# Rotated queries of the last attention, turned by VectorE and moved through DRAM instead of transposed by TensorE

## The chip, the cores and the metric

The kernel runs on one core of one Trainium2 chip. The metric is the device time of one execution in microseconds (us); the number given for a kernel is the median of its runs. The core's engines work side by side and meet at semaphores: TensorE (PE) multiplies and transposes, VectorE (DVE) and ScalarE (ACT) do elementwise work, SyncE (SP) issues almost all DMAs. Each engine takes its own instructions in the order in which they were written, and an instruction that waits holds up everything behind it on that engine.

## The reference

A float32 network over 256 tokens of width 2048, batch 1. Block one: gated linear attention and dilated attention side by side, an output projection and a gated feed-forward. Block two has two layers: retention with a convolution, then sliding-window attention with sinks. The change touches the attention of that last layer:

```python
q, k, v, gate = jnp.split(proj, ...)                 # proj = h @ w_in, 32 query heads of 64, 4 key/value heads
q = rope(rms_norm_2(q.reshape(b, s, 32, 64), q_norm_w), pos)
k = rope(rms_norm_2(k.reshape(b, s, 4, 64), k_norm_w), pos)
scores = q @ k^T * 64**-0.5                          # keys of the own 128-token block (causal) and the one before (window 128)
m = max(max(scores), sink); p = exp(scores - m); p = p / (sum(p) + exp(sink - m))
x = x + (p @ v * silu(gate)) @ w_out
```

## The kernel before

**The stream of products.** Nearly all the work is products of 256 tokens with about 340 MB of float32 weights. Each operand is cut into a high and a low part, and three products replace one. A *unit* is two k-tiles of 128 rows by 512 columns. For each unit SP loads 512 KB into one of four raw buffers, ACT writes the high part (`wh`, line 1408), DVE the low part (`wl`, line 1688), and PE runs 12 matmuls (lines 1218 to 1220), in two halves of six. There are three buffers for `wh`/`wl`: ACT can cut unit u+2 only once PE has finished unit u-1, that is when it starts unit u, and PE needs both parts two units later.

**One order for all engines.** The class `Plan` writes a single list of steps. It inserts the side work (norms, rotations, attention, splitting of activations) as *lanes*, generators that advance by half a unit (`SLOT`); `room`, `made` and `free` hold a lane back, for at most six half-units, until the planner's own table `WORK` says that an engine is free or a result is there. Each engine then walks the same list and issues its own part of each step. The list is fixed before the kernel runs; the semaphores only make an engine wait. `cut u` stands two units ahead of `mul u`.

**The last attention.** 32 query heads are worked in eight *quads* g = 0 to 7 of four heads; block j = g // 2 of the query projection (`oq`) feeds two quads. For block j:

- `oq_evac`, `on_sq` (ACT): out of PSUM into `TW`, and its squares.
- `on_rope j k` (DVE): rotation of token block k = 0, 1, three operations of 128x512 each.
- `oq_turn j k` (PE lines 1237 to 1242, ACT line 1663 on): four PE transposes of 128x128 into a bank `m`, and a copy by ACT into `qo` (in `A1`).
- `on_sum j`, `on_root j` (DVE): the sums of squares and the inverse roots by Newton steps, which scale the scores.

For quad g: `oqk g` (PE, line 1265: scores of four heads into the three `m` banks and `ob`; DVE adds the mask), `omax g` (DVE), `oexp g i` (ACT, i = 0 to 3), `oapt g i` (PE transposes the probabilities of two heads, ACT copies them, DVE makes two masked parts; i = 0, 1), `oapv g` (PE, into `ob`; ACT copies it out), `ogate g` (DVE: silu(gate) times 1/sum). The silu itself is `og j` (ACT), once per block j of the gate projection. Silu and exponential use different tables of ACT, and a change between them is an ACT_TABLE_LOAD.

The gate of a quad is turned without PE: `turn` (DVE, line 1784) transposes 32x32 pieces, `send` (SP, line 2295, four DMAs of 64 KB) writes them to a DRAM tensor `blocks`, `fetch` (SP, line 2302, one DMA of 256 KB) reads them back in the right places, and the step `msent M5 2g` multiplies with the attention's output (DVE), writes the high part `mh` (ACT) and then the low part `ml` (DVE). SP holds at a `send` until the turn is done and at a `fetch` until its four sends have landed. The output projection's units read `mh`/`ml`: unit 645 needs quad 4's, 646 quad 5's, 647 quad 6's, and 651 quad 7's. Units 629 to 644 read quads 0 to 3.

In short: the three uses of the `m` banks (`oq_turn`, `oqk`, `oapt`) take the banks in turn, and `ob` serves one head of `oqk` and all of `oapv`.

Of the kernel before, what the change touches and what calls it, by code (L numbers as in the profile page):

```python
# [103 lines left out]
def all_units(blocks):  # L104
# [15 lines left out]
    for u, un in enumerate(units):  # L120
# [28 lines left out]
        "ok_dup": (0, .8, 0), "ok_turn": (.6, 0, .45), "oq_turn": (.6, 0, .45), "og": (1.27, 0, 0)}  # L149
# [3 lines left out]
class Plan:  # L153
# [8 lines left out]
    def __init__(self, blocks, units):  # L162
        self.order, self.said, self.there, self.norms, self.emptied = [], set(), {}, 0, set()
        self.lanes = {"first": [], "att": [], "fin": [], "gate": [], "post": []}
        self.pause = dict.fromkeys(self.lanes, 0)
        self.now, self.through, self.end = 0.0, {"act": 0.0, "dve": 0.0}, {}
        self.turns, self.own, self.place, self.before = [], 0, {}, {}
        self.ring = []
        self.blocks, self.units = blocks, units
        self.lay()  # L170

    def say(self, *p):
# [23 lines left out]
        if p[0] in ("oq_turn", "oapt", "oqk"):  # L196
            self.ring += [p] * (3 if p[0] == "oqk" else 1)
# [110 lines left out]
    def after(self, b):  # L308
# [93 lines left out]
        elif kind == "oq":  # L402
# [29 lines left out]
    def turned_and_sent(self, *p):  # L432
# [11 lines left out]
        self.spawn(self.fetched(p))  # L444

# [206 lines left out]
def program(nc, t, out):  # L652
# [22 lines left out]
    by_act = ("apt", "g_kturn", "ok_turn", "oq_turn", "oapt")  # L675
# [43 lines left out]
    assert plan.turns == [q[1:] for q in plan.order if q[0] == "turn"] == list(sents)  # L719
# [10 lines left out]
    with ctx:  # L730
# [202 lines left out]
        qo = A1[:, 0:2048].rearrange("p (r h t) -> p r h t", r=2, h=4)  # L933
# [92 lines left out]
        def turn_places(p):  # L1026

            n, (group, i) = (sents[p] - 1) % 2, plan.place[p]
            if group == "r":
                return PB[:, :, 256:384], A2[:, 5128:5640].rearrange("p (i n) -> p i n", i=4)  # L1030
            first, then = {"d": (A2[:, 4096:5120], A2[:, 5120:6144]), "o": (A2[:, 2560:3584], A2[:, 3584:5632]),
# [13 lines left out]
        def sent(p):  # L1045

            n = sents[p] - 1
            return s_send[n % 2], 64 * (n // 2 + 1)

        def back(p):  # L1050

            n = sents[p] - 1
# [5 lines left out]
        def turn_place_free(p):  # L1058

            kind = p[3] if p[0] == "msent" else p[1]  # L1060
# [45 lines left out]
        def turn_source(p):  # L1106

            if p[0] == "xsent":
# [7 lines left out]
        def turn_ready(p):  # L1116

            if p[0] == "xsent":
                return x_ready(int(p[1][1]), p[2] // 4)
# [8 lines left out]
        def aw_free(*p):  # L1128
# [3 lines left out]
            return (s_turn, sents[before[-1][1:]]) if before else (s_bank, 0)  # L1132
# [13 lines left out]
        def tensor(e):  # L1146
# [8 lines left out]
            for p in plan.order:  # L1155
# [81 lines left out]
                elif kind == "oq_turn":  # L1237
                    on.wait_ge(s_orope, nth("on_rope", *a))
                    on.wait_ge(*bank_free(*p))
                    o, k = bank(*p), a[-1]  # L1240
                    four(lambda c: o[:, 128 * c:128 * c + 128],
                         lambda c: T3[:, k, 128 * c:128 * c + 128]).then_inc(s_bank, 1)
# [22 lines left out]
                elif kind == "oqk":  # L1265
                    g, j = a[0], a[0] // 2
                    on.wait_ge(*moved("oq_turn", j, 1))
                    on.wait_ge(*moved("ok_turn", 1))
                    for i in range(3):
                        on.wait_ge(*bank_free("oqk", g, i))  # L1270
                    on.wait_ge(ob_by[ob_free[p][0]], ob_free[p][1])
                    for i in (0, 2):
                        heads = [(od_bank(g, n), qo[rows_of(n), j % 2, 2 * (g % 2) + n // 2, :],
                                  ko[rows_of(n), j, :]) for n in (i, i + 1)]
                        for o, q, k in heads:
                            e.matmul(o[:, 0:128], q[:, 0:128], k[:, 0:128], start=True, stop=True)  # L1276
                        for n, (o, q, k) in enumerate(heads):
                            e.matmul(o[:, 128:384], q[:, 128:256], k[:, 0:256], start=True,  # L1278
# [118 lines left out]
        def scalar(e):  # L1397
# [18 lines left out]
            for p in plan.order:  # L1416
# [219 lines left out]
                elif kind in ("ok_evac", "oq_evac"):  # L1636
# [5 lines left out]
                    else:  # L1642
                        on.wait_ge(s_dup, 2)
                        if a[0]:
                            on.wait_ge(*full("oq_turn", a[0] - 1, 1))
# [13 lines left out]
                elif kind == "ok_turn":  # L1659
# [3 lines left out]
                         bank(*p)[:, :].rearrange("p (h t) -> p h t", h=4)).then_inc(s_bank_act, 1)  # L1663
                elif kind == "oq_turn":
                    j, k = a
                    on.wait_ge(*full(*p))
                    on.wait_ge(s_sent, sents[last_sent("xsent", "X3")])
                    if j >= 2:
                        on.wait_ge(s_pv, opened[("oqk", 2 * (j - 2) + 1)])
                    copy(qo[:, j % 2, :, 128 * k:128 * k + 128],  # L1670
# [11 lines left out]
        def vector(e):  # L1682
# [33 lines left out]
            for p in plan.order:  # L1716
# [57 lines left out]
                elif kind == "turn":  # L1774
                    n, (to, _) = sents[a], turn_places(a)
# [6 lines left out]
                    for i, part in enumerate(parts):  # L1782
                        m = slice(2 * i, 2 * i + 2) if len(parts) == 2 else slice(0, 4)
                        last = e.transpose(to.rearrange("p i (m n) -> p m i n", n=32)[:, m],
# [458 lines left out]
        def sync(e):  # L2243
# [24 lines left out]
            for p in plan.order:  # L2268
# [19 lines left out]
                elif kind == "send":  # L2288
                    n = sents[a] - 1
# [7 lines left out]
                elif kind == "fetch":  # L2297
                    n, (_, to) = sents[a] - 1, turn_places(a)
                    on.wait_ge(*sent(a))
                    if plan.before[a]:  # L2300
# [101 lines left out]
```

## Time and profile before

| | us |
|---|---|
| median of 3 runs | 1885.65 (1883.7 to 1885.96) |
| the profiled execution, whole time | 1886.98 |
| its span in the trace | 1885.1 |
| PE busy | 1876.4 (100% of the span) |
| DVE busy | 1256.0 (67%) |
| ACT busy | 996.8 (53%) |
| DMA, share of 16 engines in queue q1 | 65.0% |
| granted PE clock, mean | 0.999 |

PE's records overlap: one matmul of 128x512 is shown with 390 ns, but the next starts 0.227 us later. The starts, not the durations, give PE's pace. A gap between starts that is wider than this is time that the engine lost.

### The profile page before, as it was taken

How to read it: one execution, taken by the hardware profiler on the slowest of the kernel's cores; microseconds unless marked ns; L12 is line 12 of the kernel's file. 1: busy time of each engine (PE TensorE's matmuls, PEld its weight loads, DVE VectorE, ACT ScalarE, POOL GpSimd, SP SyncE). 2: the span in 40 equal slices, each digit the busy share in tenths (PEclk: the TensorE clock that was granted, in tenths of full speed). 3: DMA queues.
4: the chain of work that ended last, by engine and by line, in shares of the span. 5: the costliest groups of instructions: out<-in, count | busy, mean ns of one | idle time of the engine just before them, and what ended most of it. 6: DMA issues, size and time to landing. Idle time of an engine off the chain costs nothing.

```text
span 1885.1 us, 22394 instructions
## 1 busy us (share of the span) xinstructions
PE 1876.4 (100%) x8531; PEld 1545.0 (82%) x8531; DVE 1256.0 (67%) x1837; ACT 996.8 (53%) x1370; POOL 14.4 (1%) x32
## 2 busy tenths in 40 slices
PE   9999999999999999999999999999999999999999
PEld 7888888888888888888888888888888888877777
DVE  5676566776666466665466776765776676777875
ACT  6677554554444444443444465654555555566663
POOL 0001000000000000000000000000000000000000
PEclk9999999999999999999999999999999999999999
DMA  9767764686666666665666686666666577655555
GB/s 314 209 194 179 208 182 151 217 251 195 192 194 194 192 190 191 199 195 194 192 193 195 209 276 197 191 192 187 190 204 195 193 245 226 188 167 149 182 186 177
DMA packets 212362, 375.96 MB, mean 199 GB/s; under 512 B 14672, under 2 KB 35968, under 8 KB 212256
## 3 DMA queue, kind: packets, MB, share of 16 engines
q1 hardware_dynamic: 211008, 371.78, 65.0%
q0 software_dynamic: 816, 2.11, 0.8%
q8 instruction: 67, 1.10, 0.2%
q10 hardware_dynamic: 432, 0.66, 0.1%
q14 instruction: 39, 0.32, 0.0%
HBM read 361.89 MB, written 12.60 MB: 199 GB/s over the span
## 4 chain that ended last, share of the span: by engine, by line
PE 98%; DVE 1%; DMA 1%; ACT 0%; issue 0%; SPq 0%; DVEq 0%
PE g L1218 31%; PE g L1220 31%; PE g L1219 31%; PE m L1152 1%; PE ob L1296 0%; PE m L1278 0%; DMA A<-blocks 0%; DMA raw<-in_w_in 0%; PE m L1378 0%; PE m L1276 0%; PE m L1264 0%; PE ob L1364 0%; DVE wl L1688 0%; PE ob L1299 0%; PE m L1308 0%
## 5 line engine op out<-in xcount | busy, mean ns | idle before, releaser
L1688 DVE TENSOR_TENSOR wl<-raw,wh 128x1024 fp32r<-128x1024 f32 (+1 forms) x660 | 802.3, 1217 | 546.5 <-ACT wh L1408 543.2
L1408 ACT ACTIVATE wh<-raw 128x1024 fp32r<-128x1024 f32 (+1 forms) x661 | 695.0, 1052 | 721.2 <-PE g L1220 712.7
L1218 PE MATMUL g<-wh,xh 128*128 128x512 f32 x1886 | 741.7, 393 | 3.1 <-DVE wl L1688 2.7
L1220 PE MATMUL g<-wh,xl 128*128 128x512 f32 x1886 | 735.2, 390 | 0.0
L1219 PE MATMUL g<-wl,xh 128*128 128x512 f32 x1886 | 734.7, 390 | 0.0
L1218 PEld LDWEIGHTS g<-wh,xh 128*128 128x128 f32 x1886 | 354.5, 188 | 82.2 <-DVE wl L1688 5.0
L1220 PEld LDWEIGHTS g<-wh,xl 128*128 128x128 f32 x1886 | 354.3, 188 | 74.2
L1219 PEld LDWEIGHTS g<-wl,xh 128*128 128x128 f32 x1886 | 354.6, 188 | 72.1
L1218 PE MATMUL g<-wh,mh 128*128 128x512 f32 x732 | 287.6, 393 | 0.0
L1220 PE MATMUL g<-wh,ml 128*128 128x512 f32 x732 | 285.1, 389 | 0.0
L1219 PE MATMUL g<-wl,mh 128*128 128x512 f32 x732 | 284.9, 389 | 0.0
L1218 PEld LDWEIGHTS g<-wh,mh 128*128 128x128 f32 x732 | 137.4, 188 | 29.5 <-issue 1.6
L1220 PEld LDWEIGHTS g<-wh,ml 128*128 128x128 f32 x732 | 137.4, 188 | 28.8
L1219 PEld LDWEIGHTS g<-wl,mh 128*128 128x128 f32 x732 | 137.5, 188 | 28.1
L1826 DVE STREAM_TRANSPOSE A<-A 32x256 f32<-32x256 f32 x176 | 76.7, 436 | 2.9
L1688 DVE TENSOR_TENSOR x<-g,x 128x512 f32<-128x512 f32 (+1 forms) x73 | 46.4, 677 | 13.2 <-PE g L1220 7.9
L1405 ACT ACTIVATE A<-g,st 128x512 f32<-128x512 f32 x50 | 31.6, 683 | 31.3 <-PE g L1220 31.3
L1408 ACT ACTIVATE A<-TW 32x256 f32<-32x256 f32 x96 | 39.9, 416 | 1.5
L1691 DVE SCALAR_TENSOR_TENSOR xl<-A,small,xh 128x128 fp32r<-128x128 f32 (+1 forms) x112 | 34.1, 363 | 7.0 <-ACT xh L1408 7.0
L1408 ACT ACTIVATE mh<-A 128x512 fp32r<-128x512 f32 (+1 forms) x42 | 21.9, 540 | 21.1 <-DVE A L1826 16.4
L1408 ACT ACTIVATE xh<-A,small 128x256 fp32r<-128x256 f32 x64 | 28.7, 494 | 2.0 <-DMA A<-blocks 2.0
L1688 DVE TENSOR_TENSOR ml<-A,mh 128x512 fp32r<-128x512 f32 (+1 forms) x42 | 23.8, 582 | 6.8 <-ACT mh L1408 6.8
(186 smaller groups left out, 758.1 us busy)
## 6 DMA issues: line engine op xcount, KB each, us to landing
raw<-in_ev_w_in SPq DMA_DIRECT2D x128, 512.0 KB, 3.9
raw<-in_w_in SPq DMA_DIRECT2D x92, 512.0 KB, 4.3
raw<-in_w_gate SPq DMA_DIRECT2D x88, 512.0 KB, 4.4
raw<-in_w_up SPq DMA_DIRECT2D x88, 512.0 KB, 4.4
raw<-in_w_down SPq DMA_DIRECT2D x88, 512.0 KB, 4.6
raw<-in_od_w_in SPq DMA_DIRECT2D x72, 512.0 KB, 4.0
raw<-in_w_out SPq DMA_DIRECT2D x32, 512.0 KB, 4.1
raw<-in_ev_w_out SPq DMA_DIRECT2D x32, 512.0 KB, 4.7
```

The lines of the kernel that those rows point to most:

```text
L1152: last = e.transpose(dst(c), src(c), ident)
L1218: e.matmul(o, hi[:, kt, c], h, start=first, stop=False)
L1219: e.matmul(o, hi[:, kt, c], l, start=False, stop=False)
L1220: last = e.matmul(o, lo[:, kt, c], h, start=False, stop=end)
L1405: return e.activation(o, i, func, scale=scale, bias=bias)
L1408: return e.activation(o, i, AF.Copy, scale=scale)
L1688: return e.tensor_tensor(o, a, b, op)
L1691: return e.scalar_tensor_tensor(out=o, in0=a, scalar=s, in1=b, op0=op0, op1=op1)
L1826: last = e.transpose(dst, src)
```

## The change

The step `oq_turn` is gone. The rotated queries now take the way of the gates: a new pair `turn` / `send` of kind `qsent j k` behind each `on_rope j k`, and a `fetch` of at least four half-units later, straight into `qo`. This `fetch` has no splitting step behind it. DVE writes the 32x32 pieces in such an order that `qo` holds, for each token block, the four groups of heads interleaved (`p (i n)` with `n = 4n' + m`): `oqk` reads its 128 query columns of one group with a step of four elements. Sends and fetches of both kinds share the numbering of `blocks` and its semaphores (`turned_n` in place of `sents`).

Around it: `on_sum` and `on_root` of a block stand behind the second `turn`. In `oqk`, PE waits for both fetches, for banks 0 and 1 ahead of the first two heads, and for bank 2 and `ob` only ahead of the last two. In the planner, `oqk` holds until the fetch is in the list, its estimated landing (2.4 us) is over, and the previous user of `ob` is done (at most eight half-units); `oapv` holds for the previous user of `ob` as well; `og` asks for room on ACT.

```diff
-        "ok_dup": (0, .8, 0), "ok_turn": (.6, 0, .45), "oq_turn": (.6, 0, .45), "og": (1.27, 0, 0)}
+        "ok_dup": (0, .8, 0), "ok_turn": (.6, 0, .45), "og": (1.27, 0, 0)}
...
+        if p[0] in ("oqk", "oapv"):
+            self.ob = p
...
                 say("on_rope", a[0], k)
-            for k, p in enumerate(("on_sum", "on_root")):
-                yield 2 if k else 1
-                yield from self.made("on_rope", a[0], k)
-                say("oq_turn", a[0], k)
+                if k:
+                    self.sent_in_place(a[0], 0)
+            yield 1
+            yield from self.room("dve", 1.0)
+            self.sent_in_place(a[0], 1)
+            for p in ("on_sum", "on_root"):
+                yield 1
                 yield from self.room("dve", 1.0)
                 say(p, a[0])
...
             assert kind == "og"
+            yield from self.room("act", .6)
             say("og", a[0], b.i)
...
+    def sent_in_place(self, j, k):
+
+        p = ("qsent", j, k)
+        self.say("turn", *p)
+        self.say("send", *p)
+        self.place[p], self.before[p] = ("q", 0), None
+        self.turns.append(p)
+        self.spawn(self.fetched_in_place(p))
+
+    def fetched_in_place(self, p):
+
+        yield 4
+        self.say("fetch", *p)
+        self.end[("fetch",) + p] = self.now + 2.4
+        yield 1
...
     def od_quad(self, g):
         say = self.say
+        while ("fetch", "qsent", g // 2, 1) not in self.said:
+            yield 1
         for _ in range(8):
-            if (all(self.end[p] <= self.now for p in [("oq_turn", g // 2, 1)] + self.ring[-3:]) and
+            if (all(self.end[p] <= self.now for p in [("fetch", "qsent", g // 2, 1)] + self.ring[-3:] +
+                    [self.ob] * (g > 0)) and
                     self.through["dve"] - self.now <= 1.0):
                 break
             yield 1
...
+        yield from self.made(*self.ob)
         say("oapv", g)
...
                 elif kind == "oqk":
                     g, j = a[0], a[0] // 2
-                    on.wait_ge(*moved("oq_turn", j, 1))
+                    for k in range(2):
+                        on.wait_ge(*back(("qsent", j, k)))
                     on.wait_ge(*moved("ok_turn", 1))
-                    for i in range(3):
-                        on.wait_ge(*bank_free("oqk", g, i))
-                    on.wait_ge(ob_by[ob_free[p][0]], ob_free[p][1])
                     for i in (0, 2):
-                        heads = [(od_bank(g, n), qo[rows_of(n), j % 2, 2 * (g % 2) + n // 2, :],
+                        if i == 2:
+                            on.wait_ge(ob_by[ob_free[p][0]], ob_free[p][1])
+                        for n in (0, 1) if i == 0 else (2,):
+                            on.wait_ge(*bank_free("oqk", g, n))
+                        heads = [(od_bank(g, n), [qo[rows_of(n), j % 2, k].rearrange("p i (n m) -> p m (i n)", m=4)
+                                                  [:, 2 * (g % 2) + n // 2] for k in range(2)],
                                   ko[rows_of(n), j, :]) for n in (i, i + 1)]
...
-                elif kind == "oq_turn":
-                    j, k = a
-                    on.wait_ge(*full(*p))
...
+                        order = "p i (n m) -> p m i n" if a[0] == "qsent" else "p i (m n) -> p m i n"
```

The whole order of the stage moves with it. Three places are shown; line numbers of the changed kernel are about 31 higher.

**SP, around the first gate's way through DRAM** (`blocks<-A2` are the sends, `A2<-blocks` the fetch of quad 0's gate, `raw` the weight loads). Before:

```order
L1144 DMA raw<-in_od_w_in 128x2x512 [waits s_lo] x40
L2295 DMA blocks<-A2 32x4x128 [waits s_fetch0,s_turn]
L2295 DMA blocks<-A2 32x4x128 x3
L1144 DMA raw<-in_od_w_in 128x2x512 [waits s_lo] x2
L2302 DMA A2<-blocks 128x512 [waits s_send0]
```

And of the change:

```order
L2319 DMA blocks<-A2 32x4x128 [waits s_fetch0,s_turn]
L2319 DMA blocks<-A2 32x4x128 x3
L1178 DMA raw<-in_od_w_in 128x2x512 [waits s_lo] x2
L2319 DMA blocks<-A2 32x4x128 [waits s_fetch1,s_turn]
L2319 DMA blocks<-A2 32x4x128 x3
L2330 DMA A2<-blocks 128x512 [waits s_send0]
```

The sends of `qsent 2 0`, which wait for their own turn on DVE, now stand between the gate's sends and its fetch.

**ACT, at the silu of gate block 2** (`A2<-g` is `og 2`, `bias<-m0` and `A1<-m` copies out of the `m` banks, `mh<-` the step `msent`, `PB` and `st` the exponentials). Before:

```order
L1408 ACTIVATE A1<-m2 128x4x128 [waits s_bank]
L1408 ACTIVATE wh<-raw 128x1024 [waits s_mul,s_raw2]
L1405 ACT_TABLE_LOAD [waits s_gated]
L1405 ACTIVATE A2<-g0,st 128x512 [waits s_mul]
L1405 ACTIVATE A2<-g1,st 128x512
L1408 ACTIVATE wh<-raw 128x1024 [waits s_raw3]
```

And of the change:

```order
L1439 ACTIVATE mh<-AW 128x512 [waits s_oprod]
L1439 ACTIVATE wh<-raw 128x1024 [waits s_mul,s_raw3]
L1436 ACT_TABLE_LOAD
L1436 ACTIVATE A2<-g0,st 128x512 [waits s_gated]
L1436 ACTIVATE A2<-g1,st 128x512
L1439 ACTIVATE bias<-m0 128x512 [waits s_bank]
L1439 ACTIVATE wh<-raw 128x1024 [waits s_mul,s_raw0]
```

The silu now stands behind `msent M5 4` (which needs quad 2's fetch) and ahead of the copy of `oapt 3 1`, for which PE's `oapv 3` waits.

**PE, at the end of the attention** (`ob<-` is `oapv 7`). Before; the first matmul of `g0` belongs to unit 645:

```order
L1296 MATMUL ob<-PT,A1 64x256 [waits s_ob_act,s_masked]
L1296 MATMUL ob<-PT,A1 64x256
L1299 MATMUL ob<-bias,A1 64x128 x2
L1296 MATMUL ob<-bias,A1 64x256 x2
L1299 MATMUL ob<-bias,A1 64x128 x2
L1218 MATMUL g0<-wh,mh 128x512 [waits s_read_dve,s_sent,s_lo]
```

And of the change; here it belongs to unit 647:

```order
L1327 MATMUL ob<-PT,A1 64x256 [waits s_ob_act,s_masked]
L1327 MATMUL ob<-PT,A1 64x256
L1330 MATMUL ob<-bias,A1 64x128 x2
L1327 MATMUL ob<-bias,A1 64x256 x2
L1330 MATMUL ob<-bias,A1 64x128 x2
L1252 MATMUL g0<-wh,mh 128x512 [waits s_sent,s_lo]
```

Quad 7 is two units later against the products. Quad 6's `fetch` moved from behind the first half of unit 642 to behind the first half of unit 645, and its `msent` from unit 644 to directly ahead of unit 647.

## Rows read from the trace of the kernel before

**Rows 1.** The page: engines' busy time, and the two costliest groups of DVE and ACT.
```profile
PE 1876.4 (100%) x8531; PEld 1545.0 (82%) x8531; DVE 1256.0 (67%) x1837; ACT 996.8 (53%) x1370; POOL 14.4 (1%) x32
...
L1688 DVE TENSOR_TENSOR wl<-raw,wh 128x1024 fp32r<-128x1024 f32 (+1 forms) x660 | 802.3, 1217 | 546.5 <-ACT wh L1408 543.2
L1408 ACT ACTIVATE wh<-raw 128x1024 fp32r<-128x1024 f32 (+1 forms) x661 | 695.0, 1052 | 721.2 <-PE g L1220 712.7
```

**Rows 2.** Waits of PE: engine, line, releaser: total us, times, longest.
```profile
PE g L1218 <- DVE wl L1688: 2.7, 2, 2.4
...
PE m L1276 <- ACT PT L1408: 0.9, 1, 0.9
```

**Rows 3.** Timeline of PE around one `oq_turn`: start, us, engine, line.
```profile
1624.85 0.39 PE L1220 MATMUL g<-wh,xl 128*128 128x512 f32 x1
1625.08 0.60 PE L1152 MATMUL m<-small,TW 128*128 128x128 f32 x4
...
1629.62 0.39 PE L1218 MATMUL g<-wh,xh 128*128 128x512 f32 x1
```

**Rows 4.** Timeline of PE: the long gap, and an `oqk` without one.
```profile
1703.67 0.39 PE L1220 MATMUL g<-wh,xl 128*128 128x512 f32 x1
1706.44 0.50 PE L1218 MATMUL g<-wh,xh 128*128 128x512 f32 x1 [2.38 <-DVE wl L1688]
...
1709.19 0.63 PE L1219 MATMUL g<-wl,xh 128*128 128x512 f32 x1
...
1712.38 0.49 PE L1276 MATMUL m<-A 64*128 64x128 f32 x4 [0.89 <-ACT PT L1408]
...
1713.89 0.50 PE L1218 MATMUL g<-wh,xh 128*128 128x512 f32 x1
...
1735.48 0.39 PE L1220 MATMUL g<-wh,xl 128*128 128x512 f32 x1
...
1737.31 0.50 PE L1218 MATMUL g<-wh,xh 128*128 128x512 f32 x1
```

**Rows 5.** Timeline of ACT at `og 1`: silu's table load and evacuation.
```profile
1701.63 1.28 ACT L1405 ACT_TABLE_LOAD   x1
1702.92 1.26 ACT L1405 ACTIVATE A<-g,st 128x512 f32<-128x512 f32 x2
```

**Rows 6.** Timeline of DVE: `omax`, quad 6's `msent`, quad 7's `turn`.
```profile
1696.06 1.21 DVE L1697 TENSOR_REDUCE st<-PB 128x8 f32<-128x1024 f32 x1
...
1836.42 0.75 DVE L1688 TENSOR_TENSOR AW<-AW,A 128x256 f32<-128x256 f32 x2
1837.87 0.69 DVE L1688 TENSOR_TENSOR ml<-AW,mh 128x512 fp32r<-128x512 f32 x1 [0.70 <-ACT mh L1408]
...
1841.85 0.71 DVE L1784 STREAM_TRANSPOSE A<-AW 128x512 f32<-128x512 f32 x1
```

**Rows 7.** Timeline of SP: quad 6's fetch, quad 7's four sends.
```profile
1830.70 0.41 SPq L2302 DMA_DIRECT2D A<-blocks  x1
...
1842.59 1.78 SPq L2295 DMA_DIRECT2D blocks<-A  x4
```

**Rows 8.** DMA issues at 1691 us, quad 0's fetch: KB each, us to landing.
```profile
A<-blocks SPq DMA_DIRECT2D x1, 256.0 KB, 3.9
```

**Rows 9.** DMA issues from 1842 us: quad 7's sends, then its fetch.
```profile
blocks<-A SPq DMA_DIRECT2D x4, 64.0 KB, 2.9
...
A<-blocks SPq DMA_DIRECT2D x1, 256.0 KB, 5.3
```

**Rows 10.** Timeline of PE: units 642, 649, 650 and 651 begin.
```profile
1827.60 0.40 PE L1218 MATMUL g<-wh,mh 128*128 128x512 f32 x1
...
1848.81 0.39 PE L1218 MATMUL g<-wh,mh 128*128 128x512 f32 x1
...
1851.53 0.39 PE L1218 MATMUL g<-wh,mh 128*128 128x512 f32 x1
...
1854.40 0.47 PE L1218 MATMUL g<-wh,mh 128*128 128x512 f32 x1
```

More of the change, by code:

```diff
@@ L195, in say @@
             self.norms += 1
-        if p[0] in ("oq_turn", "oapt", "oqk"):
+        if p[0] in ("oqk", "oapv"):
+            self.ob = p
+        if p[0] in ("oapt", "oqk"):
             self.ring += [p] * (3 if p[0] == "oqk" else 1)
@@ L673, in find @@
         return next(p for p in plan.order if p[:len(start)] == start)
-    by_act = ("apt", "g_kturn", "ok_turn", "oq_turn", "oapt")
+    by_act = ("apt", "g_kturn", "ok_turn", "oapt")
     by_dve = ("xturn", "mix", "gates", "bias", "aqk", "g_gate", "g_at", "g_state", "r_s")
@@ L718, in program @@
     sents = {p: n + 1 for n, p in enumerate(q for q in plan.order if q[0] in ("xsent", "msent"))}
-    assert plan.turns == [q[1:] for q in plan.order if q[0] == "turn"] == list(sents)
+    assert plan.turns == [q[1:] for q in plan.order if q[0] == "turn"]
+    assert [p for p in plan.turns if p[0] != "qsent"] == list(sents)
+    turned_n = {p: n + 1 for n, p in enumerate(plan.turns)}
     ropes = {p: n + 1 for n, p in enumerate(q for q in plan.order if q[0] == "eq_rope")}
@@ L1058, in turn_place_free @@
         def turn_place_free(p):
-            kind = p[3] if p[0] == "msent" else p[1]
+            kind = {"msent": p[3:4], "xsent": p[1:2], "qsent": ("o",)}[p[0]][0]
             if kind == "d":
@@ L1106, in turn_source @@
         def turn_source(p):
+            if p[0] == "qsent":
+                return [T3[:, p[2], 0:512]]
             if p[0] == "xsent":
@@ L1116, in turn_ready @@
         def turn_ready(p):
+            if p[0] == "qsent":
+                return s_orope, nth("on_rope", p[1], p[2])
             if p[0] == "xsent":
@@ L1131, in aw_free @@
                       if q[:2] == ("turn", "msent")]
-            return (s_turn, sents[before[-1][1:]]) if before else (s_bank, 0)
+            return (s_turn, turned_n[before[-1][1:]]) if before else (s_bank, 0)
         def weights(e, u):
@@ L1236, in tensor @@
                          lambda c: src(c % 2, c // 2)).then_inc(s_bank, 1)
-                elif kind == "oq_turn":
[L1238 to L1242, printed above, removed]
                 elif kind == "bias":
@@ L1644, in scalar @@
                         if a[0]:
-                            on.wait_ge(*full("oq_turn", a[0] - 1, 1))
+                            on.wait_ge(s_turn, turned_n[("qsent", a[0] - 1, 1)])
                     evacuate(T3, b)
@@ L1783, in vector @@
                         m = slice(2 * i, 2 * i + 2) if len(parts) == 2 else slice(0, 4)
-                        last = e.transpose(to.rearrange("p i (m n) -> p m i n", n=32)[:, m],
+                        order = "p i (n m) -> p m i n" if a[0] == "qsent" else "p i (m n) -> p m i n"
+                        last = e.transpose(to.rearrange(order, n=32)[:, m],
                                            part.rearrange("p (m i n) -> p m i n", i=4, n=32))
@@ L2297, in sync @@
                 elif kind == "fetch":
-                    n, (_, to) = sents[a] - 1, turn_places(a)
+                    n, (_, to) = turned_n[a] - 1, turn_places(a)
                     on.wait_ge(*sent(a))
+                    if a[0] == "qsent":
+                        on.wait_ge(s_sent, sents[last_sent("xsent", "X3")])
+                        if a[1] >= 2:
+                            on.wait_ge(s_pv, opened[("oqk", 2 * (a[1] - 2) + 1)])
                     if plan.before[a]:
```

26 lines of the change are left out of this document (11 added, 15 removed).

## The prediction, written before the changed kernel ran

> **What bounds the kernel now.** I read the page first: PE is busy for 1876.4 of 1885.1 us, DVE 67%, ACT 53% [rows 1]. DVE's longest wait by far is for ACT's `wh`, and ACT's is for PE's matmuls [rows 1], so both run at PE's pace and PE's own work is the bound. Then PE's waits, which is where a changed order would show: in the whole run PE waited once for long on `wl` and once on ACT's copy `PT` [rows 2]. Then PE's timeline, for what one step costs. The starts are read there, since busy times overlap: units 649 and 650 begin 2.72 us apart [rows 10], 12 products with 0.227 us from start to start; I use 2.73 for a unit. Four transposes between 1624.85 and 1629.62 stretch 19 gaps (4.31 us) to 4.77 [rows 3]: a set of four costs 0.46 us.
>
> **Terms that make it faster.** (a) Eight sets of PE transposes go (four blocks, two halves each): 8 x 0.46 = 3.7 us, all on PE's path. Eight ACT copies of such a bank go too; ACT waits for PE most of the time, so I count nothing for them. (b) The stall of before. From 1703.67 to 1713.89 PE spent 10.22 us [rows 4]. In it lie 13 product gaps (2.95), four transposes (0.46) and one `oqk`. The `oqk` at 1735.48 shows what that costs without a wait: 1.83 us to the next product, less one gap, 1.60 [rows 4]. That makes 5.01, so 5.2 us are lost: 2.5 in the gap, the rest in products at the lower clock (0.43 us apart at 1709.19, the 1.2 GHz level, after an idle time of 2.38) and in `oqk` waiting for `PT`. Its cause is the order: `omax 2`, `on_root 2` and `msent 0` stand in one row on DVE, and behind it on ACT `mh`, silu's table and evacuation (1.28 + 1.26, [rows 5]) and only then `wh`. The new order takes `on_root 2` out of this row, and `oqk` no longer waits for bank 2 ahead of its first heads. I count the whole 5.2 as gone and the new order's own stalls below. Together -8.9 us.
>
> **What is added at no cost.** Eight `turn`s of 0.71 [rows 6] on DVE, 5.7 us in about 190, where DVE waits for ACT between most cuts; a turn is dear only where it delays something, and those places are priced below. Forty DMA issues on SP, 1.78 for four sends and 0.41 for a fetch [rows 7]: 8 x 2.2 = 17.5 us of SP, which otherwise waits for a free raw buffer. `oqk`'s new wait for its queries: the fetch stands at least three units (8.2 us) ahead of every `oqk` that needs it, and fetches land in 3.9 to 5.3 us [rows 8, 9]. Without this cover each of the four blocks' first quads would hold PE by up to 5 us.
>
> **Terms that make it slower.** Here I walk the new order at the three places where a chain through DRAM, DVE and ACT ends at PE. Rules: ACT can begin cut u+2 when PE begins unit u, PE needs it two units (5.5 us) later; a cut takes 1.05 on ACT and 1.22 on DVE [rows 1]; a rotation is three operations of 128x512, 0.69 each as the one that writes `ml`, `omax` a reduction of 1.21 and three small operations, about 1.7 [rows 6]; `ogate` about 1.3, exponentials of two parts about 1.05 (estimates from the same timelines). The same walk over the old order gives its stall as 2.8 us against the 2.5 seen, and no other.
>
> (c) *Quad 0's gate and `oapt 1 1`.* Zero is PE's start of unit 600; with `oapv 0` and `oapt 1 0` between, units 602, 605 and 607 start at 6.9, 15.6 and 21.0. DVE finishes cut 602 at 3.2, `omax 1` 4.9, `ogate 0` 6.2, the gate's turn 6.9, cuts 603 and 604 at 8.0 and 9.5, the rotation 11.6, the turn of `qsent 2 0` 12.2. SP must send that (1.8) before the gate's fetch, which goes out at 14.1 and lands at 17.9 to 19.4. DVE is ready for it at 16.9 and is held. Behind it in a row: the product 0.75, `mh` 0.65, `wh` of cut 607, silu 2.54, cut 608, exponential's table (another 1.28) and `oexp 1 3`: done at 26.6 or later. PE wants `oapt 1 1` at 23.8, so it idles 2.9 us, in two pieces. Then ACT's copy and DVE's masks (behind `on_sum 2`) come 1 us after PE wants `oapv 1`. With the mean landing I take 4.2. Bounds: 0, if the waits that I sum are met by slack that I don't see, and 7.3, with the slow landing and one period at the lower clock (1.9).
>
> (d) *Quad 2's gate and `oapv 3`.* Zero is the start of unit 614. The turn of `qsent 3 0` ends at 14.9, the gate's at 15.6; eight sends end at 18.5 and land 2.9 later [rows 9]; the fetch goes at 21.4 and lands at 25.2 to 26.7, while DVE could start at 23.9. Then product, `mh`, cut 623, silu with table, copy of `oapt 3 1`, masks: 0.75 + 0.65 + 1.05 + 2.54 + 0.6 + 0.76, with a little for the semaphores 6.6. So `oapv 3` can start at 32 to 33 and PE wants it at 28.7: 3.3 at the quick landing. One gap of this length is longer than the one that lowered the clock [rows 4], so I add its 1.9: 5.2. Bounds 0 and 6.5.
>
> (e) *The end.* Before, quad 6's fetch went out 3.1 us after unit 642 began (1827.60 to 1830.70), its `ml` was written at 1838.56: 11.0 us [rows 6, 7, 10]. In the new order the same chain starts from unit 645, and unit 647 needs its end. PE's way there is two units, `oapt 7 1` and `oapv 7`: 5.46 + 0.46 + 1.45 = 7.4. PE waits 3.6, or 1.8 with a landing of 3.9 instead of 5.3 [rows 8, 9]; I take 3.1. Quad 7's turn follows this step on DVE, 0.7 later. From the end of a turn to unit 651's start it was 1842.56 to 1854.40, 11.8 us [rows 6, 10]; PE's four units from 647 to 651 take 10.9. That leaves another 0.7 + 11.8 - 10.9 = 1.6. The clock may fall in the first wait, but the second then shrinks by as much. Sum 4.7, bounds 2.0 and 6.6 (DVE up to 1.4 behind at cut 647).
>
> **Sum.** -3.7 - 5.2 + 4.2 + 5.2 + 4.7 = +5.2 us. On the profiled execution's own time, 1886.98 (span 1885.1 and 1.9 around it), that is 1892.2; it ran 1.3 above the median, and on the median of 1885.65 the sum gives 1890.9. What this measurement can tell from no change is 0.2%, 3.8 us.
>
> **Rivals.**
> 1. *Faster, 1880.* DVE and ACT stay ahead of PE: (c) and (d) cost nothing because the exponentials and masks of a quad are done when PE arrives, and only the low end of (e) is paid: 1885.65 - 8.9 + 3.3. For it: PE met such a wait once in the old stage though DVE was just as full. Against it: in (c), even with the fetch landing at once, the silu and two table loads leave `oexp 1 3` 1.8 us late. It decides from (c) + (d) below 1.5 us; with (e) hidden as well 1876.8.
> 2. *No change, 1885.* The same stalls at half price: (c) 2.5, (d) 2, (e) 4 against 8.9. For it: my walk lets every duration be the full one, while packed operations on DVE start 0.1 before the last one's end is shown.
> 3. *Reading the queries with a step of four elements slows PE's weight loads.* No row shows a strided weight. An `oqk` is 16 matmuls whose loads lie side by side with them; if each load took twice as long, `oqk` would grow from 1.6 to at most 3.1, eight times: +12, to 1903. If strides cost nothing, 0, which the nearest row, the unstrided `oqk` of 1.60 [rows 4], leaves open. The Trainium skill (SBUF — State Buffer, the note on cachelines under its port mapping) says that SBUF has 16-byte lines and that each access to a new line pays; a step of four float32 is just such an access each time, although the same note calls four float32 still free. No row here decides that.
>
> **Chances.** My forecast (+3.8 to +10) 0.46; rival 1, 0.28; rival 2, 0.20; rival 3, 0.06. So faster 0.28, within 0.2% 0.20, slower 0.52. The likeliest case alone spans 1889.5 to 1896. The range has to reach into the faster case: 1879 leaves out the part of rival 1 in which (e) is hidden too, 1897 the strided reads, under 2 in 10 together.
>
> **What would show it.** Right: PE's `oqk` still about 1.6 us per quad; no stretch like 1703 to 1714 at `msent 0` with 5.2 us lost; PE idle before `oapt 1 1` and before `ob<-` of quads 1 and 3, released by ACT or by DVE's masks; PE idle at unit 647 on DVE's `ml`, 2 to 4 us, and again at 651; SP's fetch of quad 0's gate directly behind four sends. Wrong: PE's waits add up to under 5 us (rival 1); PE waits at `oqk` for DMA (the cover of three units failed); the PE weight loads of `oqk` longer than 0.19 us (rival 3); DVE's turn of a query well over 0.71 us.

## The result, and the profile after

| | before | after |
|---|---|---|
| median, us | 1885.6 (1883.7 to 1885.96, 4 runs) | 1898.46 (1895.67 to 1898.8, 4 runs) |
| ratio, 95% interval | 1 | 1.0068 [1.0056, 1.008] |
| profiled execution: time, span | 1886.98, 1885.1 | 1895.67, 1893.9 |

The change is slower by 12.9 us between the medians. The forecast was 1890.9 with a range up to 1897: right in direction, too low by 7.6 us, and outside its range. The profiled execution of after is the quickest of its four; the spans of the others are 1896.4 to 1897.0. So the traces explain 8.8 us between two spans. The other 4.1 are differences between executions: the profiled one of before was 1.3 us above its median, the profiled one of after 2.8 below.

The page of after, its engines and the two costliest groups of DVE and ACT, answers [rows 1]:

```profile
PE 1878.0 (99%) x8499; PEld 1548.6 (82%) x8499; DVE 1262.3 (67%) x1845; ACT 992.7 (52%) x1362; POOL 14.4 (1%) x32
...
L1711 DVE TENSOR_TENSOR wl<-raw,wh 128x1024 fp32r<-128x1024 f32 (+1 forms) x660 | 802.2, 1217 | 548.9 <-ACT wh L1439 545.7
L1439 ACT ACTIVATE wh<-raw 128x1024 fp32r<-128x1024 f32 (+1 forms) x661 | 695.4, 1053 | 739.4 <-PE g L1254 732.3
```

PE has 32 matmuls fewer and is busy for 1.6 us *more*. That alone tells that some of its instructions became dearer. The rest is idle time; PE's waits of after answer [rows 2]:

```profile
PE g L1252 <- DVE ml L1711: 4.9, 2, 3.0
PE ob L1327 <- DVE bias L1714: 3.6, 2, 3.0
PE m L1186 <- ACT st L1436: 1.7, 1, 1.7
...
PE g L1252 <- DVE wl L1711: 0.7, 1, 0.7
```

The waits of 2.4 for `wl` and 0.9 for `PT` are gone, and five new ones came: two for `ml` (units 647 and 651), two for the masks `bias` (`oapv 1` and `oapv 3`), one at `oapt 1 1`. The 0.7 for `wl` lies at 9 us, at the start of the kernel, where before had 0.3.

**PE's dearer instructions.** One `oqk` of after, which answers the one at 1735.48 in [rows 4]; no wait is shown in it:

```profile
1643.95 0.39 PE L1254 MATMUL g<-wh,xl 128*128 128x512 f32 x1
1644.27 0.74 PE L1307 MATMUL m<-A 64*128 64x128 f32 x4
1644.84 0.74 PE L1309 MATMUL m<-A 64*128 64x256 f32 x4
...
1646.44 0.50 PE L1252 MATMUL g<-wh,xh 128*128 128x512 f32 x1
```

From product to product it is 2.49 us, less one gap of 0.227 that is 2.26; before it was 1.60. The query is the operand that PE loads as its weights. Durations of these loads in ns (least, median, most), first of after:

```profile
L1307 PEld LDWEIGHTS m<-A x48: 304/326/328, 1644.3 to 1817.8; 64*128 64x128 f32 x48
```

The same line of before, where the 128 queries are neighbours:

```profile
L1276 PEld LDWEIGHTS m<-A x48: 182/186/187, 1644.2 to 1804.6; 64*128 64x128 f32 x48
```

All eight `oqk` grew by 0.66: **+5.3 us**.

**Term (c).** PE around `oapt 1 1` and `oapv 1`:

```profile
1701.95 0.39 PE L1254 MATMUL g<-wh,xl 128*128 128x512 f32 x1
1704.08 0.66 PE L1186 MATMUL m<-small,A 128*128 128x128 f32 x4 [1.75 <-ACT st L1436]
1704.49 0.48 PE L1252 MATMUL g<-wh,xh 128*128 128x512 f32 x1
...
1707.12 0.39 PE L1254 MATMUL g<-wh,xl 128*128 128x512 f32 x1
1708.08 0.65 PE L1327 MATMUL ob<-PT,A 128*64 128x256 f32 x4 [0.57 <-DVE bias L1714]
...
1709.53 0.50 PE L1252 MATMUL g<-wh,xh 128*128 128x512 f32 x1
```

The first piece costs 2.54 - 0.227, less 0.35 that four transposes take in steady flow: 1.96. The second costs 2.41 - 0.227 less 1.54 for an `oapv`: 0.64. Together **+2.6**. ACT in that time:

```profile
1696.44 0.63 ACT L1439 ACTIVATE mh<-AW 128x512 fp32r<-128x512 f32 x1 [2.55 <-DVE AW L1711]
1696.98 1.04 ACT L1439 ACTIVATE wh<-raw 128x1024 fp32r<-128x1024 f32 x1
1698.04 1.28 ACT L1436 ACT_TABLE_LOAD   x1
1699.34 1.27 ACT L1436 ACTIVATE A<-g,st 128x512 f32<-128x512 f32 x2
1700.49 1.06 ACT L1439 ACTIVATE wh<-raw 128x1024 fp32r<-128x1024 f32 x1
1701.57 1.28 ACT L1578 ACT_TABLE_LOAD   x1
1702.86 0.49 ACT L1578 ACTIVATE A<-A,st 128x128 f32<-128x128 f32 x1
```

This is the row of steps that the forecast walked: `mh`, `wh`, table, silu, `wh`, the other table, and only then the exponential for which PE stands still.

**Term (d).** PE at `oapv 3`:

```profile
1755.91 0.39 PE L1254 MATMUL g<-wh,xl 128*128 128x512 f32 x1
1759.33 1.12 PE L1327 MATMUL ob<-PT,A 128*64 128x256 f32 x4 [3.03 <-DVE bias L1714]
1760.24 0.64 PE L1330 MATMUL ob<-bias,A 128*64 128x128 f32 x4
...
1762.09 0.79 PE L1252 MATMUL g<-wh,xh 128*128 128x512 f32 x1
```

6.18 - 0.227 - 1.54 is 4.4, and 0.3 in the two products behind it: **+4.7**. Of it 3.0 is the wait; the rest is `oapv` itself, which took 2.8 us instead of 1.45 after the idle time. There the granted clock fell: it is 0.73 from 1760 to 1765, and 1.00 in the same 5 us of the second trace (e1 below), where the same `oapv` took 1.45 and the whole place cost 2.9. DVE just before waited for quad 2's fetch:

```profile
1753.05 0.76 DVE L1711 TENSOR_TENSOR AW<-AW,A 128x256 f32<-128x256 f32 x2 [1.96 <-DMA A<-blocks]
```

**Term (e).** PE at units 647 and 651, which answers the end of [rows 10]:

```profile
1843.54 0.40 PE L1254 MATMUL g<-wh,ml 128*128 128x512 f32 x1
...
1848.56 0.77 PE L1252 MATMUL g<-wh,mh 128*128 128x512 f32 x1 [3.00 <-DVE ml L1711]
1849.12 0.63 PE L1253 MATMUL g<-wl,mh 128*128 128x512 f32 x1
1849.54 0.63 PE L1254 MATMUL g<-wh,ml 128*128 128x512 f32 x1
...
1860.69 0.39 PE L1254 MATMUL g<-wh,ml 128*128 128x512 f32 x1
1862.98 0.47 PE L1252 MATMUL g<-wh,mh 128*128 128x512 f32 x1 [1.90 <-DVE ml L1711]
```

Lost are 4.79 less `oapv`'s 1.54 at the first wait (3.25), 1.3 in six products up to 0.56 apart behind it (granted clock 0.50, the 1.2 GHz level), and 2.06 at the second: **+6.6**. On DVE the masks and the gate of quad 7 and a cut stand ahead of quad 6's gate product (`AW` at 1846.27, with no idle time before it). The fetch for this product went out at 1841.13, behind two weight loads, and landed 5.09 us later, at 1846.22. So DVE's row and the fetch were ready within 0.1 us of each other; in e1 DVE waits 0.27 for the fetch. Neither alone is the cause.

```profile
1838.33 2.65 SPq L1178 DMA_DIRECT2D raw<-in_od_w_out  x2
1841.13 0.36 SPq L2330 DMA_DIRECT2D A<-blocks  x1
```

The second wait has another cause. Quad 7's fetch went out at 1855.85 and landed 4.1 us later, at 1859.94, and DVE took it only 0.75 us later. What came last is the cut ahead of quad 7's gate product (`TE`) in DVE's row; ACT could start this cut's `wh` only when PE began unit 650, at 1858.20:

```profile
1846.27 0.75 DVE L1711 TENSOR_TENSOR AW<-AW,A 128x256 f32<-128x256 f32 x2
...
1859.55 1.23 DVE L1711 TENSOR_TENSOR wl<-raw,wh 128x1024 fp32r<-128x1024 f32 x1 [1.50 <-ACT wh L1439]
1860.69 0.76 DVE L1711 TENSOR_TENSOR TE<-TE,A 128x256 f32<-128x256 f32 x2
```

From there the rest (`wh`, `wl`, product, `mh`, `ml`) is fixed work, and PE wants `ml` one unit after it began unit 650. In before the product stood one cut earlier, behind the one released by unit 649, and PE lost 0.15. The wait is 1.90 in each of the traces of after, e1, e2, e3, e5 and e7, in none of which DVE waits for this fetch. The fetch itself is late by SP's order, not by the memory: its sends had landed at 1852.15, but a weight load stands ahead of it that got its raw buffer only at 1855.34. So one cut earlier alone would gain at most 0.75 (0.17 in e7).

Sum of the traces: -3.7 (transposes) - 5.2 (old stall) + 5.3 + 2.6 + 4.7 + 6.6 = +10.3. The spans differ by 8.8; 1.3 us of the rest is that this execution of after was that much earlier already at 1611, ahead of all changed work (a transpose stands at 1611.69, in before at 1613.00).

### The profile page after: what moved, and what is told of

It reads as the page before. It is cut to its first block, busy times and chain, and to the rows that moved or that the text cites. A ratio compares the mean times of both kernels' runs of the same rounds, so it can differ in the third digit from the quotient of the medians.

```text
span 1893.9 us, 22385 instructions
## 1 busy us (share of the span) xinstructions
PE 1878.0 (99%) x8499; PEld 1548.6 (82%) x8499; DVE 1262.3 (67%) x1845; ACT 992.7 (52%) x1362; POOL 14.4 (1%) x32
## 4 chain that ended last, share of the span: by engine, by line
PE 95%; DVE 1%; ACT 1%; DMA 1%; issue 1%; SPq 0%; DVEq 0%; ACTq 0%
PE g L1252 31%; PE g L1254 30%; PE g L1253 30%; DMA A<-blocks 1%; ACT wh L1439 0%; DVE wl L1711 0%; PE m L1309 0%; PE m L1307 0%; PE m L1186 0%; PE ob L1327 0%; DMA raw<-in_w_in 0%; PE m L1409 0%; SPq L2319 0%; DVE st L1720 0%; PE m L1292 0%
```

## The experiments

The kernel before was run beside all of them. All numbers are medians unless a span is named; "idle" is PE's wait as the trace shows it.

| run | median (range, runs) | ratio to before [95%] | span |
|---|---|---|---|
| e1 changed kernel again | 1897.02 (1) | | 1895.2 |
| e2 contiguous read | 1892.33 (1891.69 to 1895.28, 5) | 1.0038 [1.0025, 1.0051] | 1890.2 |
| e3 no silu | 1891.28 (1889.52 to 1893.83, 6) | 1.003 [1.0018, 1.0042] | 1887.9 |
| e4 packed by the fetch | 1893.0 (1890.82 to 1895.01, 5) | 1.0038 [1.0024, 1.0052] | 1890.6 |
| e5 silu later | 1892.22 (1891.62 to 1894.12, 4) | 1.0039 [1.0024, 1.0054] | 1890.2 |
| e6 quads' pace | 1889.36 (1887.84 to 1891.31, 10) | 1.0022 [1.0012, 1.0031] | 1886.4 |
| e7 all repairs | 1884.87 (1883.62 to 1886.22, 10) | 0.9998 [0.9988, 1.0007] | 1881.8 |
| e8 before, step of four | 1889.87 (1888.69 to 1891.47, 9) | 1.0026 [1.0016, 1.0036] | 1887.4 |
| e9 all repairs and fetches | 1884.62 (1882.97 to 1885.55, 11) | 0.9995 [0.9986, 1.0004] | 1883.7 |
| e10 before, silu later | 1881.45 (1881.02 to 1882.6, 11) | 0.9981 [0.9973, 0.999] | 1879.6 |
| e11 before, split waits | 1883.58 (1) | | 1881.7 |
| e12 before, step of two | 1884.46 (1) | | 1882.6 |

**e1, the changed kernel once more.** No edit.

> The changed kernel once more, for a second profile. Its timed runs were 1895.7 once and 1898.2 to 1898.8 three times, and the profile is of the 1895.7. Theory A (PE's waits at the three late chains, plus slower reads of the queries): the same waits at the same steps (before oapt 1 1, oapv 1, oapv 3, units 647 and 651), each within 0.5 us, oqk 2.26 us instead of 1.60; a run of 1898 differs from the one of 1895.7 only in products at the 1.2 GHz level behind one of the gaps, 1.9 us at a time. Rival B (the 40 additional DMAs disturb the weight loads): waits on raw buffers or wl appear at other places in the second profile.

The waits came back within 0.4 us (`ml` 3.4 and 1.9, `bias` 2.8, `oapt` 1.7), so they belong to the order. No wait for weights came at a new place, so the 40 additional DMAs did not hold the stream of products. What moved is the clock: 19 intervals of 0.43 us between products, against 5 in the first trace. The slow period of `oapv 3` is gone (1.9 us less there), and (e) cost 9.9 us instead of 6.6, with slow products behind both of its waits.

**e2, the read alone.** `oqk` reads 128 neighbours of what the same fetch wrote, and nothing else differs:

```diff
-                        heads = [(od_bank(g, n), [qo[rows_of(n), j % 2, k].rearrange("p i (n m) -> p m (i n)", m=4)
-                                                  [:, 2 * (g % 2) + n // 2] for k in range(2)],
+                        heads = [(od_bank(g, n), [qo[rows_of(n), j % 2, k].rearrange("p i n -> p (i n)")
+                                                  [:, 128 * (2 * (g % 2) + n // 2):128 * (2 * (g % 2) + n // 2) + 128]
+                                                  for k in range(2)],
```

> The changed kernel, but oqk reads 128 neighbouring elements of qo instead of every fourth: same number of matmuls, same shapes, same moves; it thereby mixes heads and tokens, so the scores are other numbers. Theory A: oqk falls from 2.26 to 1.60 us at PE, eight times 0.66, so 5.3 us less than the changed kernel (1893 beside 1898.5), and the waits at oapt 1 1, oapv 1, oapv 3, 647, 651 stay or grow by what PE arrives earlier. Rival B (DMAs are the cost): within 1 us of the changed kernel.

Every `oqk` is back at 1.60 us and its loads at 188 ns. But the span fell by 3.7, not by 5.3: the wait at `oapv 3` grew from 3.0 to 5.0. PE came there 3.5 us earlier, the chain only 1.5, since DVE now waited 3.49 us for quad 2's fetch instead of 1.96.

**e3, the silu out.** The last attention's gate enters without its silu, so neither the function nor its table loads are there:

```diff
-evacuate(so[:, j % 2, :, :], a[-1], AF.Silu)
+evacuate(so[:, j % 2, :, :], a[-1])
```

> The changed kernel with the gate's silu in the last attention left out (a plain scaled copy): no table loads of 1.28 us before and behind each og. Theory A: oexp 1 3 is 2.56 us earlier and so PE's wait before oapt 1 1 (1.75 us of idle) goes, with it most of the one before oapv 1; the copy of oapt 3 1 is 1.28 us earlier, so the 3.03 us before oapv 3 fall to about 1.7; waits at 647 and 651 stay at 3.0 and 1.9. Together 3 to 5 us less than the changed kernel, with clock periods. Rival C (these two waits come from the fetches of the gates, not from ACT's queue): both waits stay within 0.5 us.

The idle times at `oapt 1 1` and `oapv 1` are gone and the one at `oapv 3` fell from 3.03 to 1.31; the end is as it was. The walk of (c) and (d) holds: silu and its tables make them, and 1.3 of (d) is left without it, for which DVE's wait for the fetch, 1.66 in this trace, is the likely cause.

**e4, packed on the way.** The transposes write neighbours, and four fetches of 64 KB in runs of 128 bytes take the place of the one, so that the contiguous read gets the right queries:

```diff
-                        order = "p i (n m) -> p m i n" if a[0] == "qsent" else "p i (m n) -> p m i n"
+                        order = "p i (m n) -> p m i n"
...
+                    if a[0] == "qsent":
+                        for i in range(4):
+                            e.dma_start(to.rearrange("p i n -> p (i n)").rearrange("p (m i n) -> p i m n", m=4, i=4)[:, i],
+                                        memory[n % 4].rearrange("p (i m n) -> p i m n", i=4, m=4)[:, i]
+                                        ).then_inc(s_fetch[n % 4], 16)
```

> The changed kernel with the queries laid out packed and still right: DVE writes its pieces as for the gates, and each query fetch is four DMAs of 64 KB with runs of 128 bytes that put the four groups of heads side by side; oqk reads 128 neighbouring elements. Theory A: oqk 1.60 us, so -5.3 us at PE, less what the 24 more issues on SP (0.43 us each) delay: 1893 to 1896. Rival D (short runs make the fetches so slow that they hold SP and oqk): PE waits at oqk for DMA, slower than the changed kernel.

It does what e2 does, within the measurement, with the right queries. The idle time at `oapv 3` is 5.1, and PE waits for no DMA at `oqk`.

**e5, the silu later.**

```diff
             yield from self.room("act", .6)
+            while a[0] in (1, 2) and ("oapv", 2 * a[0] - 1) not in self.said:
+                yield 1
             say("og", a[0], b.i)
```

> The changed kernel; only the silu steps of gate blocks 1 and 2 are held in the list until oapv 1 and oapv 3 stand in it (the strided queries stay). Theory: PE's idle times ahead of oapt 1 1, oapv 1 and oapv 3 (1.75 + 0.57 + 3.03 us) come from the silu and its two table loads standing between the gate's msent and the exponentials. Then those at oapt 1 1 and oapv 1 go, the one at oapv 3 shrinks to about 1 (the wait for the fetch is left), the end of the attention stays as it is: 1898.5 - 5 = 1893. Rival: the fetch alone makes these waits, the silu only stands in the same place: then all three stay within 1 us and the time is 1897 to 1899. Against both: quads move, since the lanes behind the silu move with it, and a new wait may come where the silu now stands.

(c) and (d) are gone but for 0.2. Three new waits of 0.9 us each came at other `oapt` (once for `st`, twice for `PB`), where the silu now stands. The gain of 3.7 between the spans is about the 7.1 gained at the old places less three times 1.15 at the new.

**e6, the pace of the quads.**

```diff
-        while ("fetch", "qsent", g // 2, 1) not in self.said:
+        while ("fetch", "qsent", g // 2, 1) not in self.said or (g and ("omax", g - 1) not in self.said):
             yield 1
...
             say("oexp", g, i)
-            yield 2
+            yield 1
```

> The changed kernel with the pace of the quads mended: oqk g is held until omax g-1 is in the list (it overtook omax 1 at quad 2), and an exponential is followed by one half-unit instead of two. Quad 6's msent then stands at unit 645.0 instead of 646.5, quad 7's at 650.0 instead of 650.5; the strided queries stay. Theory: the waits of units 647 and 651 for ml come from the two units by which the quads are late: 3.0 goes to nearly 0, 1.9 to 1 or less, 4 to 5 us gained at the end; what is between oapt 1 1 and oapv 3 changes by 2 us either way. 1893.5. Rival: the chain of a quad through memory is itself too long and moves with PE, so that both waits stay within 0.5 us: 1897 to 1899.

Better than expected by 4 us. The wait of unit 647 is gone; that of unit 651 became 2.8. PE's waits:

```profile
PE g L1252 <- DVE ml L1711: 2.8, 1, 2.8
...
PE m L1186 <- ACT PB L1578: 0.8, 1, 0.8
PE ob L1327 <- DVE bias L1714: 0.7, 1, 0.7
PE g L1252 <- DVE wl L1711: 0.5, 1, 0.5
PE m L1186 <- ACT A L1578: 0.4, 1, 0.4
```

So the first wait of (e) comes from quad 6 being two units late, as forecast. The second did not go: 1.9 of its 2.8 is the place of quad 7's gate product in the list, as above, and the rest DVE's wait of 0.84 for the fetch. And the middle got cheaper as well: (c) and (d), 7.3 us, became five small stalls of 3.4 us in all. My reading is that `omax 1`, now ahead of `oqk 2`, lets quad 1 be done when quad 0's gate comes; no run isolates it.

**e7, all together** (e4, e5 and e6 in one).

> All repairs together: queries packed by four small fetches so that oqk reads 128 neighbouring elements (worth 5.3 us), silu of blocks 1 and 2 behind oapv 1 and 3 (up to 6), quads paced as in the run before (4 to 5 at the end). If the terms add: 1898.5 - 16 = 1882.5, 3 us under the kernel before. If they only trade waits, as when the contiguous read alone lengthened the wait ahead of oapv 3 from 2.8 to 5.1: 1888 to 1892. If each wait really goes, what is left of the change is its gain of 8.9 us: 1877 to 1878.

```profile
PE g L1254 <- DVE ml L1714: 1.9, 1, 1.9
...
PE ob L1330 <- DVE bias L1717: 1.4, 1, 1.4
PE m L1188 <- ACT PB L1581: 1.4, 1, 1.4
PE g L1254 <- DVE wl L1714: 0.6, 1, 0.6
PE m L1188 <- ACT A L1581: 0.6, 1, 0.6
```

13.6 us of the 16 hoped for, and with them the change is even with the kernel before: most of what the transposes and the old stall give is eaten by 5.9 us of waits that are left.

**e8, the step of four in the kernel before.** The old order, the old way; only the layout of `qo`:

```diff
-        qo = A1[:, 0:2048].rearrange("p (r h t) -> p r h t", r=2, h=4)
+        qo = A1[:, 0:2048].rearrange("p (r k t h) -> p r k t h", r=2, k=2, h=4)
```

> The kernel before, its order untouched, with the transposed queries laid out so that oqk reads them with a step of four elements (ACT's copy writes them with that step). Theory: the step costs 0.66 us in each of eight oqk, whatever wrote the queries: 1885.7 + 5.3 = 1891, and oqk takes 2.26 instead of 1.60. Rival: the longer oqk of the changed kernel comes from something else of its order or of the fetch into the same memory: then oqk stays at 1.60 and the time at 1885.7. If ACT's strided write also got slower than its 0.6 us, that would be hidden beside PE.

Its loads take what they take in the changed kernel:

```profile
L1276 PEld LDWEIGHTS m<-A x48: 304/326/327, 1643.0 to 1806.7; 64*128 64x128 f32 x48
```

Every `oqk` outside the old stall is 2.26 instead of 1.60. The median is 4.3 higher, where eight times 0.66 is 5.3; the interval (3.0 to 6.8 us) holds both. The cost is the step's alone, whoever wrote the queries.

**e9, fetches in another order.** e7, with the queries' fetches of blocks 1 to 3 two units later and the gates' `msent` of quads 0 to 2 one unit later:

```diff
-        yield 4
+        yield 8 if p[1] else 4
...
-        yield 6 if p[0] == "xsent" else 4
+        yield 6 if p[0] == "xsent" else 6 if p[:2] == ("msent", "M5") and p[3] == "o" and p[4] < 3 else 4
```

> All repairs together as in the run e7, and two more: the queries' fetches of blocks 1 to 3 stand two units later in SP's list (behind the gate's fetch), and the gates' msent of quads 0 to 2 one unit later, since DVE waited 1.7 us for quad 0's fetch. Theory: of the 5.8 us that PE still waited, the 1.4 ahead of oapv 1 and part of the 1.4 ahead of oapt goes, the 1.9 at unit 651 stays: 1884.9 - 2 to 3 = 1882.5, under the kernel before by 3 (0.16%), which may be too little to tell. Rival: the waits are of DVE's and ACT's work, not of the fetch: 1884 to 1886, no change.

The wait ahead of `oapv 1` went, one at a later `oapt`, for ACT's exponential, grew from 0.6 to 1.7, and the one at unit 651 from 1.9 to 2.3, with DVE 0.3 us late for its fetch. No change. Waits were only traded.

**e10, the kernel before without its stall.**

```diff
             assert kind == "og"
+            while a[0] == 1 and ("oexp", 2, 3) not in self.said:
+                yield 1
             say("og", a[0], b.i)
```

and `oqk`'s waits split as in the change.

> The kernel before with two small edits and nothing of the way through memory: the silu of gate block 1 is held in the list until oexp 2 3 stands in it (unit 609.5 instead of 604.5), and oqk waits for bank 2 and ob only ahead of its last two heads. Theory: the old stall of 5.2 us is this silu with its table load between mh and wh, and goes: 1885.6 - 5 = 1880.6. Rival: omax 2, on_root 2 and msent 0 in one row on DVE and the fetch of quad 0 make it as well: then 2 to 3 of the 5.2 stay, 1883.

```profile
PE m L1162 <- DVE wl L1746: 1.5, 1, 1.5
PE ob L1299 <- DVE bias L1694: 0.5, 1, 0.5
```

Both waits of [rows 2] are gone, for one of 0.5; the 1.5 at L1162 lies outside the stage and is in all kernels. This is the quickest of all: 17 us under the changed kernel's median, and faster than before by 0.19%, with an interval that excludes 1. The 5.2 us came to 3.6 by the ratio (3.3 between the medians), with 0.5 of wait left.

**e11, the split waits alone.**

```diff
-                    for i in range(3):
-                        on.wait_ge(*bank_free("oqk", g, i))
-                    on.wait_ge(ob_by[ob_free[p][0]], ob_free[p][1])
                     for i in (0, 2):
+                        if i == 2:
+                            on.wait_ge(ob_by[ob_free[p][0]], ob_free[p][1])
+                        for n in (0, 1) if i == 0 else (2,):
+                            on.wait_ge(*bank_free("oqk", g, n))
```

> The kernel before; only oqk's waits are split (banks 0 and 1 ahead of the first two heads, bank 2 and ob ahead of the last two). Theory: of the old stall only the 0.9 us in which oqk 2 waits for ACT's copy PT goes, the gap of 2.4 at wl stays: 1885. Rival: the split takes the whole second half of the stall (2.5 of 5.2): 1883.

The 0.9 at `oqk 2` went, the gap of 2.4 stayed. It ran once, so its 1883.58 tells little.

**e12, a step of two.** As e8, with two groups interleaved instead of four.

> The kernel before, its order untouched, its queries laid out so that oqk reads them with a step of two elements (8 bytes) in place of one; a step of four made an oqk 2.26 instead of 1.60. If the cost follows the number of bytes passed over, 1.8 us each and +1.7 in all (1887); if only steps of 16 bytes and more pay, 1.60 and 1885.7; if any step pays the same, 2.26 and 1890.

```profile
L1276 PEld LDWEIGHTS m<-A x48: 189/193/194, 1643.0 to 1802.1; 64*128 64x128 f32 x48
```

7 ns more per load, and an `oqk` at 1.63. Between a step of two and one of four lies nearly the whole cost; a step of three was not run. The spans of e8 and e12, the same order with no slow product in either, differ by 4.8 us, for eight times 0.63.

## Why the prediction was wrong

**The step that failed is a term put at nothing: rival 3.** "Reading the queries with a step of four elements slows PE's weight loads" had a chance of 0.06 and stood in the sum with 0. It was true, at 0.66 us per `oqk`, 5.3 in all. Two errors are in that. Its size: I had only the ceiling of 1.5 per `oqk` and nothing between. And its place: it was set up as another outcome beside the forecast, although it excludes none of the terms and would have come on top of every one. With 5.3 added to the terms as I had them, the forecast is 1896.2, and the measured 1898.46 is 2.3 away. Part of that nearness is luck: (c) and (d) were 2.1 too high together and (e) 1.9 too low. The prediction had named the sign, loads longer than 0.19 us; they were 0.326.

The Trainium skill (SBUF — State Buffer, the note on cachelines under port mapping) says both that a 16-byte line needs at least two hits for full bandwidth and that four fp32 can be stepped over for free. The runs agree with the first and not with the second: two hits per line (step of two) 193 ns, one hit (step of four) 326, neighbours 186.

**Term by term.**

- (a) -3.7: held. No row of a query transpose is left on PE.
- (b) -5.2: the stall went, but its price was partly luck. The 2.4 for `wl` and 0.9 for `PT` are in the traces of e12 as well, yet there no product of the stage was at the lower clock (granted 1.00 from 1705 to 1710). In the profile of before the granted clock was 0.56 from 1706.5 to 1710, seven products lay 0.43 apart, and the products behind the gap lost 1.6. Taking the stall away gained 3.6 in e10, not 5.2. The order's stall is worth about 3.6, and 1.6 of my -8.9 was the clock of one execution.
- (c) +4.2, measured 2.6. The chain is the forecast's (e3 and e5 take it away), but quad 0's fetch hardly held DVE: issued at 1692.80, it landed 2.8 us later, and DVE, free 0.1 earlier, used it at 1695.64. I had counted 3.8 to 5.3 for a landing.
- (d) +5.2, measured 4.7: a wait of 3.0 against 3.3, and the clock, 1.7 against 1.9. In e1 the wait is 2.8 and the clock costs nothing, so its share of this agreement is luck.
- (e) +4.7, measured 6.6, its upper bound. The first wait, 3.0 against 3.1, is the forecast's, though DVE's row was as late as the fetch. The second, 1.9 against 1.6, is right by luck. I had it from the chain through memory, a turn to unit 651's start in 11.8 us; measured are 14.0, and the fetch landed 0.75 us before DVE took it. What holds PE is the cut ahead of quad 7's gate product, which starts only when PE has begun unit 650. So "the clock may fall in the first wait, but the second then shrinks by as much" failed: six slow products lost 1.3 (in e1 the slow products behind both waits 4.2), and the second wait stayed at 1.90, since it moves with PE.
- "A turn of 0.71": the queries' turns (`A<-TW`) took 1.08 us, 3.0 more on DVE in all, against 0.70 for the gates' (`A<-AW`) on the same line of after, and against 0.70 in e7, where neighbours are written. They stand in the rows behind (c) and (d), and their share of those waits isn't separated:

```profile
L1808 DVE STREAM_TRANSPOSE A<-AW x12: 681/704/712, 162.6 to 1848.3; 128x512 f32<-128x512 f32 x12
L1808 DVE STREAM_TRANSPOSE A<-TW x8: 1053/1084/1094, 1625.6 to 1750.0; 128x512 f32<-128x512 f32 x8
```

- The cover of `oqk` held: no PE wait for a DMA at any quad. Rival 1, which wanted (c) + (d) below 1.5, is refuted by 7.3 us. Rival 2 had (c) right (2.5 against 2.6), but wanted 2 and 4 for (d) and (e), which are 4.7 and 6.6.
- Two sums of the prediction do not come out of its rows. In (e) a landing of 3.9 instead of 5.3 takes 1.4 off 3.6, which leaves 2.2 and not 1.8; that moves the forecast by 0.2 at most. Rival 1 adds 3.3 for the low end of (e), whose bound is given as 2.0.

**What stays open.** Why the other executions of after took 2.5 to 3.1 us longer than the profiled one. The granted clock was 0.998 in the profiled execution of after and 0.996 to 0.997 in the three others, and e1, at 0.997 and 19 slow intervals, was 1.3 us longer with waits that agree within 0.4 us. That points to clock periods in and behind the new gaps, though not to every gap: e6, with its wait of 2.8, shows no slow product in the stage. It is not shown for the three executions that have no trace. Nor was any run made with quad 7's gate product one cut earlier and its fetch ahead of that weight load, by which the rows above would shorten the wait of 1.90.

## What to carry to other kernels

A cost that would come on top of every case is a term of the sum with its bounds, not a rival with a chance of its own. Moving work off the bounding engine buys only what that engine spent on it (here 3.7 us), so first look whether the stall beside it goes by a small edit of the order, as in e10. A wait whose length is the same in many runs (1.90 here) points to a place in the list and not to a transfer. And a stall read from one execution includes what the clock did behind it: the wait came back in every trace, the slow products behind it did not.

## What the runs showed of the hardware

- A weight load of 64x128 float32 took 186 ns from neighbouring elements, 193 with a step of two and 326 with a step of four; sixteen of them with their matmuls 1.60, 1.63 and 2.26 us.
- Writing with a step of four is dear on the other engines too: DVE's 32x32 transposes of 128x512 took 1.08 us instead of 0.70, and in e8 ACT's copies of 128x512 out of PSUM 1.09 (the median of its group) instead of 0.60.
- The same gap of 2.4 us on PE was followed by seven products 0.43 us apart in the profile of before, and by none in those of e8, e11 and e12.
